# A decoder step with block-sparse attention: samples as 128x128 tiles, prompt heads in pairs, one-pass penalty, capped key loads

## What is computed

```python
h = rms(x, g_pre); z = h @ w_in                      # 1024 -> 7 chunks of 512
ua, va, ga, qb, kb, vb, gb = split(z)
# group A: 4 groups x 128 channels
a = gelu(ua) * (tril(W_s) @ rms_group(gelu(va)) + b_s)    # in chunks of 128 positions
# group B: 8 heads x 64, blocks of 256 keys: the 3 past blocks with the
# largest q . mean(k), and the own block; causal; scores minus slope_h * distance
o = softmax(q k^T / 8 - slope_h * dist) v
y = concat(rms(a) * silu(ga), rms(o) * silu(gb)) @ w_out
out = x + rms(y, g_post)
```

## Time and profile before

| | |
|---|---|
| median of three runs | 470.17 us (469.98 to 471.4) |
| profiled execution, span from first to last instruction | 515.1 us |
| profiled execution, its time around the span | not recorded |
| mean granted clock of PE, profiled execution | 0.923 |
| DMA | 110.95 MB, mean 215 GB/s over the span |

### The profile page before, as it was taken

How to read it: one execution, slowest core, us unless ns; L and a number is a source line. 1 busy time by engine, 2 the same in 40 slices (tenths; PEclk the granted TensorE clock), 3 DMA queues, 4 the chain that set the end, 5 groups by cost and what they waited for, 6 DMA issues and landing times.

```text
span 515.1 us, 7913 instructions
## 1 busy us (share of the span) xinstructions
PE 436.1 (85%) x2264; PEld 192.2 (37%) x2264; DVE 281.0 (55%) x749; ACT 124.9 (24%) x290; POOL 242.3 (47%) x356
## 2 busy tenths in 40 slices
PE   6989983999389985999739997799798997798993
PEld 3423431343034532555324543234333343243430
DVE  1535732366055764969445585559542674658253
ACT  2411100000123524553222544142122111000112
POOL 5875277105840054911763117862578357517111
PEclk9989997999699985999955999899999998899998
DMA  8995499545996069911998009993899169924121
GB/s 286 400 394 180 165 382 380 74 165 164 391 283 204 7 198 296 288 15 43 341 391 187 1 22 342 382 335 87 270 303 360 24 232 373 327 30 106 63 81 43
DMA packets 76698, 110.95 MB, mean 215 GB/s; under 512 B 44568, under 2 KB 45080, under 8 KB 76656
## 3 DMA queue, kind: packets, MB, share of 16 engines
q0 software_dynamic: 22576, 71.45, 39.6%
q1 hardware_dynamic: 42720, 21.14, 16.5%
q10 hardware_dynamic: 11360, 17.86, 10.3%
HBM read 106.11 MB, written 4.29 MB: 214 GB/s over the span
## 4 chain that ended last, share of the span: by engine, by line
PE 36%; DVE 14%; another core or an unknown queue 13%; DMA 12%; issue 9%; POOL 8%; ACT 2%; DVEq 2%; ACTq 1%; SPq 1%; POOLq 0%
PE PA L957 17%; DMA K<-in_cache_k,kidx 10%; POOL K L820 6%; PE PA L1047 5%; PE GB L1063 5%; DVE ksum L1492 3%; PE SB L1003 3%; PE PO L1024 2%; DMA V<-in_page_table 1%; DVE ksum L684 1%; PE SB L1012 1%; POOL rstd L834 1%; PE SB L911 1%; DVEq L1490 1%
## 5 line engine op out<-in xcount | busy, mean ns | idle before, releaser
L820 POOL DMA_INDIRECT K<-in_cache_k,kidx x128 | 128.3, 1002 | 146.3 <-DVE ksum L1492 110.8
L957 PE MATMUL PA<-wbuf,hT 128*128 128x512 f32 x384 | 189.0, 634 | 0.0
L684 DVE TENSOR_TENSOR ksum<-K 128x512 f32<-128x512 f32 x128 | 85.1, 688 | 72.3 <-DMA K<-in_cache_k,kidx 54.2
L957 PEld LDWEIGHTS PA<-wbuf,hT 128*128 128x128 f32 x384 | 72.1, 200 | 94.7 <-issue 93.6
L669 POOL DMA_DIRECT2D V<-in_cache_v x128 | 75.5, 594 | 49.9 <-issue 38.9
L1047 PE MATMUL PA<-wbuf,hT 128*128 128x512 f32 x128 | 61.6, 622 | 0.1
L1063 PE MATMUL GB<-ksum,win 128*32 128x512 f32 x256 | 39.6, 675 | 16.4 <-DVE ksum L684 12.3
L1492 DVE TENSOR_TENSOR ksum<-K,qb 128x128 f32<-128x128 f32 x192 | 42.0, 286 | 11.4 <-issue 5.9
L833 POOL TENSOR_SCALAR rstd<-msum 128x1 f32<-128x1 f32 (+3 forms) x24 | 7.9, 330 | 62.3 <-ACT junk L1136 36.6
L1047 PEld LDWEIGHTS PA<-wbuf,hT 128*128 128x128 f32 x128 | 23.3, 194 | 28.3 <-issue 27.7
L1024 PE MATMUL PO<-v,pT 128*128 128x64 f32 x160 | 23.9, 284 | 7.9 <-DVE yb L1410 7.4
(11 more groups left out here) (186 smaller groups left out, 377.7 us busy)
## 6 DMA issues: line engine op xcount, KB each, us to landing
wbuf<-in_w_in ACTq DMA_DIRECT2D x5, 2048.0 KB
V<-in_cache_v SPq DMA_DIRECT2D x240, 32.0 KB
V<-in_cache_v POOLq DMA_DIRECT2D x128, 32.0 KB, 6.3
wbuf<-in_w_out ACTq DMA_DIRECT2D x2, 2048.0 KB
wbuf<-in_w_in SPq DMA_DIRECT2D x4, 512.0 KB, 8.2
wbuf<-in_w_in SPq DMA_DIRECT2D x1, 2048.0 KB
K<-in_cache_k,kidx POOLq DMA_INDIRECT x128, 12.6
qb<-q_rows SPq DMA_DIRECT2D x8, 256.0 KB
```

What stands on the lines that cost most here:

```text
L684: eng.tensor_tensor(ksum[:, n % SUMS, :], K[:, n, 0, :], K[:, n, 1, :], ALU.add).then_inc(s_dsum, 1)
L820: pool.indirect_dma_start(K[:, n, :, :].rearrange("p r w -> p (r w)"), None, k_rows, bass.IndirectOffsetOnAxis(ap=kidx[:, b, n:n + 1], axis=0)
L957: last = pe.matmul(bank[:, :], lhs, rhs, start=(kc == 0), stop=(kc == KC - 1))
```

## The change

- *Samples.* A projection forms, for each group j of 32 array columns, the sum over all eight input chunks for 128 of the 512 columns: 32 matmuls of 128 columns in place of 8 of 512. The result lies as 128 partitions (group, sample) by 128 columns, without a fold; ACT evacuates it in one step, with the function applied. All later sample steps work on 128x128. Sums over a sample's four groups are small matmuls with a 0/1 matrix (`ra`, `fin1`, `ffd`; `rs` spreads the scale). Tables for this layout come by 20 DMAs on SP ahead of the first value fetches, and each store of the samples is four DMAs. The copy of denominators to one row, and their DMA, fall away.
- *Prompt heads in pairs.* `qk` does two heads on rows 0 to 63 and 64 to 127 of the array, into two SB banks. `pv` has the values stationary (64 columns) and the transposed probabilities streaming, two heads in column groups 0 to 63 and 64 to 127; the result is transposed, so ACT copies it, PE turns it (`turn`), and DVE scales it.
- *One pass.* One DVE instruction adds penalty and scores, scales and keeps the minimum, in place of two passes. q is scaled by 1/slope for that, and the exp step takes scale -1.
- *Key loads.* `load_k` waits until the block five before has landed (`AHEAD = 5`).
- *Order.* The gate chunk gb has buffers of its own and its matmuls don't wait for attention any more; the turn has a lane of its own on PE ahead of attention; the residual rows are loaded by SP's queue, not ACT's.

```diff
-SQUARED = {"pj": ("va", "ga", "gb"), "sfd": ("va", "ga")}
+SQUARED = {"pj": ("va", "ga", "gb"), "spj": ("va", "ga")}
+AHEAD = 5
+PAIRS = H // 2
...
             first = [("Q", ("w", c))] if c else [("DVE", ("xn", t))]
-            if name == "gb":
-                first.append(("DVE", ("pv", H - 1, NT - 1)))
...
+    if m >= AHEAD:
+        bb, nn = divmod(m - AHEAD, NB)
+        pool.wait_ge(s_k[nn], 16 * (bb + 1))
     pool.indirect_dma_start(K[:, n, :, :]...)
...
-            def sample_partials(s, w, src):
+            def sample_columns(s, w, src):
                 bank = sb_begin(pe, s)
                 for kc in range(KC):
-                    j = kc % 4
-                    last = pe.matmul(bank[32 * j:32 * j + 32, :], src[:, kc, :], w[:, kc, :],
-                                     start=(kc < 4), stop=(kc >= 4), tile_position=(0, 32 * j))
+                    for j in range(G):
+                        last = pe.matmul(bank[32 * j:32 * j + 32, 0:P], src[:, kc, :], w[:, kc, j * P:(j + 1) * P],
+                                         start=(kc == 0), stop=(kc == KC - 1), tile_position=(0, 32 * j))
...
-                elif kind in ("sfd", "ffd"):
-                    sb_filled(pe.matmul(bank[0:B, :], fold[:, :], spart[:, :], start=True, stop=True), s)
...
+                    pair = [sb_begin(pe, s + (hh,)) for hh in range(2)]
+                    for hh in range(2):
+                        o = HD * hh
+                        sb_filled(pe.matmul(pair[hh][:, 0:(i + 1) * P], qT[o:o + HD, p, i * P:(i + 1) * P],
+                                            kT[o:o + HD, p, 0:(i + 1) * P], start=True, stop=True,
+                                            tile_position=(o, 0)), s + (hh,))
...
                     for jt in range(i + 1):
-                        last = pe.matmul(PO[:, i * HD:(i + 1) * HD], pT[:, a % 2, jt, :],
-                                         v[:, jt, h * HD:(h + 1) * HD], start=(jt == 0), stop=(jt == i))
+                        for hh in range(2):
+                            h = 2 * p + hh
+                            last = pe.matmul(PO[HD * hh:HD * hh + HD, i * P:(i + 1) * P], v[:, jt, h * HD:(h + 1) * HD],
+                                             pT[:, a % 2, hh, jt, :], start=(jt == 0), stop=(jt == i),
+                                             tile_position=(0, HD * hh))
...
+                elif kind == "turn":
+                    pe.wait_ge(po_free, p + 1)
+                    for i in range(NT):
+                        last = pe.transpose(bank[:, i * P:(i + 1) * P], oT[:, i * P:(i + 1) * P], ident[:, :])
...
-                    sb_emptied(dve.scalar_tensor_tensor(out=pr[:, a % 2, 0:m], in0=alibi[:, SEQ - m:SEQ], scalar=SLOPES[h],
-                                                        in1=sb_bank(s)[:, 0:m], op0=ALU.mult, op1=ALU.add), s)
-                    dve.tensor_reduce(smax[:, a % 2:a % 2 + 1], pr[:, a % 2, 0:m], AX.X, ALU.max,
-                                      negate=True).then_inc(s_pmax, 1)
+                        last = dve.tensor_tensor_reduce(out=pr[:, a % 2, hh, 0:m], in0=alibi[:, SEQ - m:SEQ],
+                                                        in1=sb_bank(s + (hh,))[:, 0:m], scale=-SLOPES[2 * p + hh],
+                                                        scalar=BIG, op0=ALU.add, op1=ALU.min,
+                                                        accum_out=smin[:, a % 2, hh:hh + 1])
...
-                if kind == "res":
-                    act.wait_ge(s_ptused, H * NT)
+                elif kind == "res":
+                    sp.wait_ge(s_ptused, PAIRS * NT)
+                    sp.wait_ge(s_vrow_stored, 16 * (NT + G))
```

More of the change, by code:

```diff
@@ L39 @@
 PARTS = 4
+AHEAD = 5
+PAIRS = H // 2
+HEAD = [2 * (x % 4) + x // 4 for x in range(H)]
+BIG = 3.0e38
 def v_queue(b, k):
@@ L49, in make_plan @@
 def make_plan():
-    pairs = [(h, i) for h in range(H) for i in range(NT)]
+    pairs = [(p, i) for p in range(PAIRS) for i in range(NT)]
     last = QUARTERS - 1
@@ L62, in add @@
         needs[eng, s] = deps
-    for eng, names in (("PE", "gate score first attention side sample project"), ("ACT", "square score exp turn sample side evacuate fetch"),
-                       ("DVE", "first " + DVE_LANES), ("POOL", POOL_LANES), ("SP", "spread rows fetch gather"),
+    for eng, names in (("PE", "gate score first turned attention side sample project"), ("ACT", "square score exp turn sample side evacuate fetch"),
+                       ("DVE", "first " + DVE_LANES), ("POOL", POOL_LANES), ("SP", "spread rows residual fetch gather"),
                        ("Q", "key value weight")):
@@ L73, in spj @@
     def spj(c):
+        name = CHUNKS[c]
         weights = [("Q", ("w", c))] if c else [("Q", ("w0", x)) for x in range(QUARTERS)]
[L75 to L85, removed]
+        add("PE", "sample", ("spj", c), 1.9, *weights, *([] if c else [("DVE", ("xs",)), ("PE", ("rs",))]))
@@ L114, in make_plan @@
             add("DVE", "first", ("xs",), 0.3, ("PE", ("xs",)))
+            add("PE", "first", ("rs",), 0.3, ("POOL", ("xs",)))
+            add("DVE", "first", ("rs",), 0.2, ("PE", ("rs",)))
     for c in range(len(CHUNKS)):
         spj(c)
-        sfd(c)
         name = CHUNKS[c]
@@ L186, in out @@
         add("ACT", "evacuate", ("op", t, half), 0.8, ("PE", ("op", t, half)))
-        add("DVE", "out", ("op", t, half), 0.8, ("ACT", ("op", t, half)), ("ACT", ("res",)))
+        add("DVE", "out", ("op", t, half), 0.8, ("ACT", ("op", t, half)), ("SP", ("res",)))
         if half == 1:
@@ L214, in make_plan @@
[L214 to L215 removed]
+            p, i = pairs[a - 1]
+            for hh in range(2):
+                s = ("ptr", p, i, hh)
+                add("PE", "attention", s, 0.1 + 0.13 * (i + 1), ("ACT", ("qk", p, i)))
+                deps = [("PE", ("pv",) + pairs[a - 3])] if a >= 3 else []
+                add("ACT", "turn", s, 0.25 + 0.11 * (i + 1), ("PE", s), *deps)
         if a >= 2:
[L217 removed]
@@ L218, in make_plan @@
-            s = ("pv", h, i)
-            deps = [("DVE", ("pv", h - 1, NT - 1))] if i == 0 and h >= 1 else []
-            add("PE", "attention", s, 0.36 * (i + 1), ("ACT", ("ptr", h, i)), *deps)
+            p, i = pairs[a - 2]
+            s = ("pv", p, i)
+            deps = [("ACT", ("out", p - 1))] if i == 0 and p >= 1 else []
+            add("PE", "attention", s, 0.15 + 0.25 * (i + 1), ("ACT", ("ptr", p, i, 1)), *deps)
             if i == NT - 1:
-                add("DVE", "norm", s, 0.7, ("PE", s), *([("SP", ("krow", NT))] if h == 0 else []))
@@ L223, in make_plan @@
-    add("ACT", "fetch", ("res",), 2.5, ("PE", ("pv", H - 1, NT - 1)), ("SP", ("vrow", NT)))
+                add("ACT", "turn", ("out", p), 0.65, ("PE", s), *([("PE", ("turn", p - 1))] if p else []))
+                add("PE", "turned", ("turn", p), 0.6, ("ACT", ("out", p)))
+                add("DVE", "norm", ("turn", p), 0.95, ("PE", ("turn", p)), *([("SP", ("krow", NT))] if p == 0 else []))
+    add("SP", "residual", ("res",), 2.5, ("PE", ("pv", PAIRS - 1, NT - 1)), ("SP", ("vrow", NT)))
     for b in range(B):
@@ new lines, in make_plan @@
+    add("POOL", "tiny", ("fin1",), 1.0, ("DVE", ("fin1",)))
+    add("DVE", "tail", ("fin2",), 0.4, ("POOL", ("fin1",)))
+    add("PE", "score", ("fin2",), 0.4, ("DVE", ("fin2",)))
+    add("DVE", "tail", ("fin2b",), 0.3, ("PE", ("fin2",)))
+    for half in range(2):
+        add("PE", "score", ("fop", half), 1.9, ("DVE", ("fin2b",)))
+        add("ACT", "score", ("fop", half), 0.9, ("PE", ("fop", half)))
+    add("PE", "score", ("ffd",), 0.3, ("ACT", ("fop", 1)))
+    add("DVE", "tail", ("ffd", 0), 0.2, ("PE", ("ffd",)))
@@ L294, in make_plan @@
+    add("POOL", "tiny", ("ffd",), 1.0, ("DVE", ("ffd", 0)))
+    add("DVE", "tail", ("ffd", 1), 0.9, ("POOL", ("ffd",)))
     banks = {"pa": [], "sb": [], "dc": []}
@@ L323, in make_plan @@
                 kind, size, _ = bank(s)
-                if len(banks[kind]) >= size:
-                    deps.append(banks[kind][-size])
+                held = 2 if s[0] in ("qk", "xn") else 1
+                for back in range(size - held + 1, size + 1):
+                    if len(banks[kind]) >= back:
+                        deps.append(banks[kind][-back])
             if any(d not in ends for d in deps):
```

574 lines of the change are left out of this document (326 added, 248 removed).

## The result

The changed kernel takes 449.3 us (median of its runs) against 470.8 for the kernel before beside it: a ratio of 0.953 (95% interval 0.948 to 0.959). The forecast was 448. The time is right; the reason given for it holds only in part.

A forecast was written before the change was run, and what follows sets the result against it. The prediction took a full TensorE, broken by holes while key blocks load, as the bound. TensorE's -24.0 us and the end's -1.0, less 2.9 of the folds, made -22 from 470.2: 448 us, range 440 to 456 (0.45).

The forecast's parts named there:

- What bounds the kernel: Whole span: a full TensorE, broken by holes while key blocks load; work taken off it counts nearly in full.
- must be mostly holes and the half clock: First profile of the kernel before: its 45 us over the runs' median are TensorE standing still and the lower clock afterwards.
- PE's terms: TensorE: folds -8.6, sample projections 0, scores -11.7, values -7.0, turns +2.0, group sums +1.3; together -24.0 us.
- rival 4: Paired heads on TensorE don't overlap: only 4 to 8 us gained, 464 us; 0.20 together with another rival.
- One pass: VectorE's penalty and minimum joined: 15.6 us of passes go, counted as 0, with up to 5 us gained.
- hidden by PE's work: VectorE, at 55% busy: its saved pass pays only where the selection of blocks queues behind attention.
- The cap: Key loads, five blocks on their way: 0, with no loss as long as a block lands within about 6.6 us.
- SyncE's tables: 20 table loads ahead of the first sample's values, which come 20 us later: 0, up to 10 us once if uncovered.
- The end: The 7.6 us behind the last matmul: -1 us, bounds -3 to +2.
- The sum: Whole kernel: -25.0 us, less 2.9 of the folds where keys set the pace, gives -22 and 448 us.
- Rival 2: Key loads, not TensorE, set the pace: only 1 to 10 us gained, 462 us; 0.20 together with another rival.
- rival 3: The cap starves key loads: blocks land after 9 us, one every 1.8, costing 38 us, 486 us; chance 0.12.

The follow-up runs named there:

- the planned cut: Kernel before with every second input chunk left out of each projection's last prompt tile, and the planner told of it: 466.3 us, ratio 0.992.
- the second profile of before: The kernel before, unchanged, profiled once more beside the experiments: span 471.4 us, its own time 473.1.

## Why the prediction was right, and where its reasons were not

- *What bounds the kernel.* Wrong as put. PE is full, but 24.5 us less of it gained 0 and 4.7 us before, and 0 after. Two chains lie within some 10 us of each other: PE's list, and eight rounds of loading, choosing and scoring. The change shortened both. Either alone should have given little: the planned cut gained 4.7 by less PE work, and with PE's work put back everything else in the change, the cap's loss among it, left 478.6. That the first profile's excess "must be mostly holes and the half clock" was right.
- *PE's terms.* Right. Slots summed over the second profile of before and the one after: folds 7.8 us away (forecast 8.6), sample projections 18.2 to 20.3 (+2.1, taken as 0, bound +3), scores 24.7 to 11.9 (-12.8, forecast -11.7), values 20.1 to 11.2 (-8.9, forecast -7.0), turns +2.0, sums +1.7 (forecast +1.3). Together -23.7, forecast -24.0. The other 13 us of PE's busy time are mostly the same matmuls run less often at the lower clock: by the trace's record of the granted clock 36.1 us of PE's busy time lay at the lower level before and 15.2 lie there after, which makes about 10 us. The prediction had no term for this; its mark for PE's busy time, near 412, was missed for it (391.7), and because it started from the disturbed profile. Timeline of PE after, answering:

```profile
209.12 1.98 PE L1034 MATMUL PA<-wbuf,hT 128*128 128x512 f32 x4
211.03 1.13 PE L1088 MATMUL SB<-kT,qT 64*128 64x512 f32 x4
212.09 0.55 PE L1097 MATMUL SB<-ident,pr 128*128 128x128 f32 x3
...
227.39 1.95 PE L978 MATMUL SB<-wbuf,hTs 128*32 128x128 f32 x64
229.28 1.98 PE L1034 MATMUL PA<-wbuf,hT 128*128 128x512 f32 x4
```

  Four score records of 512 columns take 212.09 - 211.03 = 1.06 us, where two of one head were forecast at 1.05: two row groups stream together, and rival 4 is out. The Trainium skill (TensorEngine Tiling, Key Properties) says that tiles run independently; here the trace agrees. A sample projection with 64 records takes 1.89.
- *One pass.* Mis-sized: 0 with up to 5, measured 6.2. The step that failed is "hidden by PE's work": DVE's steps of the choice are in the samples' round, and PE covers nothing there.
- *The cap.* Mis-sized: 0, measured 7.2 lost. Its rule (a cost from 6.6 us of landing on) held at 8.0 us; I took the engines' pace of 1.31 us a block, not the landing under five. That pace was read from two sums of the first sample; for samples 1 to 7 the key sums came every 1.92 us on average in the second profile before, 1.83 after and 1.77 without the cap.
- *SyncE's tables.* Right: the 20 loads were issued from 44.2 to 54.7, and the first value page at 61.5; nobody waited. But a wait that I had not named came in at the same place (timeline of POOL, DVE and PE after):

```profile
37.02 0.93 POOL L872 DMA_INDIRECT K<-in_cache_k,kidx  x1 [0.44 <-DMA K<-in_cache_k,kidx]
37.95 0.13 POOL L920 MEMSET group<- 128x4 f32 x1
...
38.73 0.32 POOL L923 MEMSET xs<- 128x256 f32 x1
...
39.08 0.29 DVE L1466 TENSOR_TENSOR mix<-qs,ks 128x128 f32<-128x128 f32 x1 [4.56 <-POOL xs L923]
...
40.49 0.20 PE L1150 MATMUL DC<-fold,snw 128*8 128x8 f32 x2 [4.30 <-DVE snw L1468]
```

  POOL clears the samples' tables behind sixteen key loads; DVE stands 4.56 us for it ahead of its key sums (3.17 without the cap), and PE 4.30. I put most of the 5.3 us lost until sample 1's first load down to it; no run moved the tables.
- *The end.* Mis-sized: -1, while the stretch behind the last key sum is 10.8 shorter. Where the samples end last in both (the planned cut, and after), from the last value sums to the end took 30.8 and 23.1 us. I put these 7.7 us down to the new layout of the samples; no run shows it alone.
- *The order.* The gate chunk's wait was not priced at all; without it the kernel is probably faster, by 3.3 us (medians) to about 7 (ratios).
- *The sum.* PE's 24, counted as 22, came to the right time because terms that I had at nothing cancelled: gains in the choice, at the end and at the clock against the cap's 7 and the 5 at the start. That 448 was hit is in good part luck. Rival 2's mark (PE's busy time falls by 20 and the span doesn't follow) came true where the kernel before was cut, not here; rival 3's (key sums every 1.8 us or more) came true on average (1.83) but tells nothing of the cap, since without it they came every 1.77 and before every 1.92.

No run undid the samples' layout alone, kept the weight loads away from the keys with all else as it was, or held the clock. So it is shown that PE's work alone didn't set the time and that the samples' rounds set it after the change; how the 21.5 us gained divide among the parts stays open.

## What to carry to other kernels

An engine that is 85 to 91% busy is not yet the bound: cut some of its work, change nothing else, and see whether the time moves. Where two chains lie close, an edit pays only as far as the other chain lets it, and putting work back tells more than taking more away. Read the granted clock beside both: here the cut and the return of TensorE's work each moved it. For a cap on loads in flight, landing time over issue interval is a first guess (here, as an estimate, 9.4 / 1.32, about 7): eight was free, five cost 1.6%, six and seven were not run, and without the cap or with eight the changed kernel takes 442 and 441 us, better than both.

## What the runs showed that was not expected

- A 2 MB weight load lands after 9.3 to 10.8 us (medians) in the profile after, where most fall between the key bursts, and after 16.1 to 22.4 in the second one before, where most fall into them; with the cap, a burst with such a load in it took 36.4 to 39.5 us, and one without 32.4 to 33.0. Whether the change paid partly by moving these loads is not shown apart.
- One profiled execution of the same kernel spanned 515.1 us and another 471.4; the longest gaps of PE were 9 and 4.6 us.
- The joint DVE instruction takes 684 ns at 512 columns, as long as one of the two passes that it replaces.
